# Branch C's attention steps in a 2-layer hybrid decoder: two places a unit instead of three, and a map factor made by one fused instruction

## What is computed

```python
def diff_attention(q, k, v, lam):
    """q,k [B,T,H,2,32]; v [B,T,H,64]; lam scalar -> (softmax1 - lam*softmax2) v, [B,T,H,64]."""
    ...
        s = jnp.einsum('bqhcd,bkhcd->bhcqk', qb, k).astype(jnp.float32) * scale
        p = jax.nn.softmax(jnp.where(causal, s, -jnp.inf), axis=-1)
        pd = (p[:, :, 0] - lam * p[:, :, 1]).astype(v.dtype)
        return jnp.einsum('bhqk,bkhd->bqhd', pd, v)
...
u = jnp.einsum('btnc,ncd->btnd', y, w_branch)
g = jax.nn.sigmoid(pr['g'].reshape(b, t, N_BRANCH, d))
out = jnp.sum(g * u, axis=2) @ w_out
return layer_norm(DN_ALPHA * x + out, ln_g, ln_b)
```

## Time and profile before

| | us |
|---|---|
| median of 3 runs | 1393.51 |
| lowest and highest | 1391.75, 1394.14 |
| the profiled execution | 1390.51 |
| its span | 1388.9 |
| PE busy | 1325.7 (95%) |
| DVE busy | 655.3 (47%) |
| ACT busy | 651.6 (47%) |
| POOL busy | 674.3 (49%) |

### The profile page before, as it was taken

How to read it: one execution, slowest core, us unless ns; L and a number is a source line. 1 busy time by engine, 2 the same in 40 slices (tenths; PEclk the granted TensorE clock), 3 DMA queues, 4 the chain that set the end, 5 groups by cost and what they waited for, 6 DMA issues and landing times.

```text
span 1388.9 us, 19055 instructions
## 1 busy us (share of the span) xinstructions
PE 1325.7 (95%) x6872; PEld 1126.4 (81%) x6872; DVE 655.3 (47%) x1641; ACT 651.6 (47%) x1296; POOL 674.3 (49%) x850
## 2 busy tenths in 40 slices
PE   6999999999999999999999989999999999999995
PEld 5977788888877898888888778888888779888884
DVE  4567746433146553213365774763322675432044
ACT  4455345454276464433245533554524764553232
POOL 3543353354565354467374325424446533645764
PEclk9999999999999999999999999999999999999998
DMA  7322242221331143242322113322124212323221
GB/s 263 109 74 62 70 114 68 65 74 62 103 95 38 39 119 106 58 121 76 119 76 86 61 61 88 95 76 74 57 64 116 61 45 80 96 58 106 84 76 60
DMA packets 147052, 116.47 MB, mean 84 GB/s; under 512 B 5520, under 2 KB 131856, under 8 KB 146704
## 3 DMA queue, kind: packets, MB, share of 16 engines
q1 hardware_dynamic: 146816, 114.22, 27.6%
q10 hardware_dynamic: 144, 1.05, 0.2%
HBM read 112.10 MB, written 3.15 MB: 83 GB/s over the span
## 4 chain that ended last, share of the span: by engine, by line
PE 81%; DVE 10%; ACT 4%; issue 2%; POOL 1%; DMA 1%; SPq 0%; POOLq 0%; DVEq 0%; ACTq 0%
PE product L729 20%; PE product L730 19%; PE product L731 19%; PE context L969 4%; PE scores L941 3%; PE branch_product L729 3%; PE branch_product L731 3%; PE branch_product L730 3%; PE transposed L954 3%; DVE probabilities L1398 1%; DVE index_scores L1364 1%; ACT score_operands L993 1%; DMA residual<-in_x_dram 1%; DVE index_scores L1375 1%; POOL residual L671 1%
## 5 line engine op out<-in xcount | busy, mean ns | idle before, releaser
L713 POOL TENSOR_TENSOR weights_rest<-raw_weights,weights_head 128x320 fp32r<-128x320 f32 (+3 forms) x672 | 544.3, 843 | 387.1 <-ACT weights_head L993 387.1
L729 PE MATMUL product<-weights_head,stationary_head 128*128 128x512 f32 (+3 forms) x768 | 291.2, 379 | 5.9 <-POOL weights_rest L713 5.8
L993 ACT ACTIVATE weights_head<-raw_weights 128x1280 fp32r<-128x1280 f32 (+4 forms) x178 | 198.1, 1114 | 206.6 <-PE product L731 160.9
L730 PE MATMUL product<-weights_rest,stationary_head 128*128 128x512 f32 (+3 forms) x768 | 286.0, 372 | 0.0
L731 PE MATMUL product<-weights_head,stationary_rest 128*128 128x512 f32 (+3 forms) x768 | 285.8, 372 | 0.0
L729 PE MATMUL product<-stationary_head,weights_head 128*128 128x512 f32 x640 | 260.6, 407 | 0.0
L730 PE MATMUL product<-stationary_rest,weights_head 128*128 128x512 f32 x640 | 250.4, 391 | 0.0
L731 PE MATMUL product<-stationary_head,weights_rest 128*128 128x512 f32 x640 | 250.4, 391 | 0.0
L698 POOL TENSOR_TENSOR merged<-merged,activated 128x256 f32<-128x256 f32 x128 | 93.2, 750 | 276.0 <-DVE activated L1519 275.9
L729 PEld LDWEIGHTS product<-weights_head,stationary_head 128*128 128x128 f32 x768 | 145.5, 189 | 27.6 <-POOL weights_rest L713 6.6
L1104 ACT ACTIVATE probabilities<-probabilities,negated_maxima 128x256 f32<-128x256 f32 (+3 forms) x160 | 86.3, 539 | 172.9 <-DVE negated_maxima L1398 172.2
(11 more groups left out here) (201 smaller groups left out, 1809.0 us busy)
## 6 DMA issues: line engine op xcount, KB each, us to landing
raw_weights<-in_w_in_dram SPq DMA_DIRECT2D x104, 512.0 KB, 3.7
raw_weights<-in_w_in_dram SPq DMA_DIRECT2D x72, 256.0 KB, 2.9
raw_weights<-in_w_branch_dram SPq DMA_DIRECT2D x80, 128.0 KB, 3.7
raw_weights<-in_w_out_dram SPq DMA_DIRECT2D x16, 512.0 KB, 3.6
merged<-in_w_mem_kv_dram SPq DMA_DIRECT2D x8, 512.0 KB, 7.3
raw_weights<-in_w_in_dram SPq DMA_DIRECT2D x8, 416.0 KB, 3.1
raw_weights<-in_w_in_dram SPq DMA_DIRECT2D x8, 296.0 KB, 3.9
residual<-in_x_dram SPq DMA_DIRECT2D x4, 512.0 KB, 10.7
```

The costliest lines, as they stand in the source:

```text
L713: ins = nc.gpsimd.tensor_tensor(WL[:, sw, part], RAW[:, sr, part], WH[:, sw, part].bitcast(F32), ALU.subtract)
L729: nc.tensor.matmul(dst, sh, mh, start=start, stop=False)
L730: nc.tensor.matmul(dst, sh, ml, start=False, stop=False)
L993: return nc.scalar.activation(dst, src, ACT.Copy, scale=scale)
```

## The change

The second and third place of a unit become one, so a unit has two places. The stretch of C's list ends one group of D0 later. The first factor step and the multiplication by lambda become one scalar_tensor_tensor: (1/r1 x lambda) x r0.

```diff
@@ diff_steps
         if j < NH and m < 2 and i < UNITS:
             third.append(("ev", "C", j, m))
             late = [("er", "C", j, m)]
-        out += [first, second, third]
+        out += [first, second + third]
     return out
@@ PLACES
-    ("C attention", ("gA0", 0, 0), ("D0", 3, 1), 0.0),
+    ("C attention", ("gA0", 0, 0), ("D0", 3, 2), 0.0),
@@ the join on DVE
                         chain(nc.vector.reciprocal(f[1], rs[1]))
-                        chain(nc.vector.tensor_tensor(f[0], f[1], rs[0], ALU.mult))
-                        chain(nc.vector.tensor_tensor(f[1], f[0], LAM[:, 4:5], ALU.mult))
-                        nc.vector.scalar_tensor_tensor(out=first, in0=second, scalar=f[1], in1=first, op0=ALU.mult,
+                        chain(nc.vector.scalar_tensor_tensor(out=f[0], in0=f[1], scalar=LAM[:, 4:5], in1=rs[0], op0=ALU.mult,
+                                                             op1=ALU.mult))
+                        nc.vector.scalar_tensor_tensor(out=first, in0=second, scalar=f[0], in1=first, op0=ALU.mult,
                                                        op1=ALU.add).then_inc(joined.sem, note(joined, step))
```

## The result

| | before | changed |
|---|---|---|
| median, us | 1392.63 | 1400.66 |
| lowest and highest, us | 1388.57, 1394.14 | 1400.04, 1402.86 |
| the profiled execution, us | 1390.51 | 1400.29 |
| its span, us | 1388.9 | 1398.7 |

The ratio is 1.0067, with a 95% interval of 1.0048 to 1.0087. The change made the kernel slower by 8 us. The forecast was 1394.9 us, from 1390.3 to 1398.4; it counted from a median before of 1393.51 us, and the one measured beside the changed kernel is 1392.63.

What follows compares the result with a forecast made beforehand. PE, busy 95% of the span, was taken as the bound. Old waits of 9.8 us a layer give way to 10.5, so +0.7 a layer and +1.4 on the median 1393.51: 1394.9 us, range 1390.3 to 1398.4.

Steps and rivals of the forecast that it cites:

- What bounds the kernel: Whole kernel: PE is busy 95% of the span, so time is lost or won where PE stands still.
- What goes: C's attention: the old waits for exits, joins and remainders leave their old places, a loss of 9.8 us a layer.
- What comes: C's attention: new waits at joins 0, 2, 4, 6, 8, following exits, remainders and the normaliser, 10.5 us a layer.
- ACT's 0.25: Units 2 and 6: ACT's remainder copies ahead of L1165 make L1519 0 to 0.6 us late, taken as 0.25 twice.
- second rival: ACT's copies hold L1519 at two places in each layer: 2.8 us more, 1397.7 us; chance 0.24.
- the sign of the forecast: PE in C's stretches: idle time near 7.6 us again, one of the signs that the forecast is right.
- The sum: C's attention, both layers: +0.7 us a layer, so +1.4 for the kernel, from -2 to +4.4.
- The waits' cost: PE's waits in C: start-to-start excess, 0.6 and 1.15 us at shared places, 0.2 more than their idle time.
- The fused step: DVE's joins in C: one factor step takes 0.20 us free and 0.77 behind L1519.
- The first rival: Five joins behind L1519 slip past POOL's pieces: 1385.6 us, or about 1390 with one delay gone; chance 0.16.
- The range: Kernel time to hold 8 in 10: 1390.3 to 1398.4 us, to the first rival's weak form and the second.

Runs made afterwards that it cites:

- the pauses filled: The changed kernel with matmuls of no use put into PE's long waits, before the transposes of units 2 and 6 and maps 8 and 16: 1394.96 us.
- the order alone: The changed kernel's order with the old join of two factor steps instead of the fused one: 1412.92 us, ratio 1.0138 to the kernel before.
- join first: The changed kernel with the join one place earlier, in the first place of the unit behind the even map's exit: 1384.57 us, ratio 0.9944.
- three places, new end: The changed kernel with three places a unit again, keeping the fused join and the stretch one group longer: 1381.98 us, ratio 0.9944.
- filled before maps 8 and 16: The changed kernel with 12 matmuls of no use before each of these two maps only, transpose pauses left empty: 1394.18 us, ratio 1.0017.
- remainders earlier: The changed kernel with q and k of each head prepared one unit earlier (ACT's copies and branch C's remainders): 1395.15 us, ratio 1.0025.
- join first, remainders earlier: The changed kernel with the join in the first place and the preparation one unit earlier: 1381.45 us, ratio 0.9930.

## Why the prediction was wrong

**What bounds the kernel** held: PE, so that time is lost or won where it stands still. That it can also run slower was left out.

**What goes** held. All 8 waits for exits are gone from their places but a rest at map 15 (0.17 us idle in layer 1, none in layer 0), and so are those at joins 11 and 13 and map 24.

**What comes** held in place, and in size but for unit 2. The waits stand at transposes 0, 2, 4, 6, 8 and maps 8, 16, where they were forecast. Forecast and measured (idle plus 0.16): 1.35 and 1.24 at unit 0; 1.10, with ACT's 0.25 1.35, and 1.94 at unit 2; 1.35 and 1.21 at unit 6; 1.8 and 1.70 at map 8; 0.52 and 0.41 at units 4 and 8; 0.7 and 0.59 at map 23. The join behind L1519 took 0.71 + 1.05 us where 0.77 + 1.12 was said: one wait for POOL in each, as worked out from the earlier trace rows. At unit 2 the term that was too small was ACT's: L1519 came 1.45 us after the last branch matmul, so 0.95 late, where I took 0.25 of a bound of 0.6; at unit 6 it was 0.58 late. The copies of 2.42 us ended at 414.02 and L1165 followed at 414.04:

```profile
411.60 2.42 ACT L993 ACTIVATE score_operands<-product 32x512 fp32r<-32x512 f32 x4
414.04 0.60 ACT L1165 ACTIVATE activated<-product 128x512 f32<-128x512 f32 x1
```

That is the second rival's mechanism, and at unit 2 its size too: 0.7 beyond what was taken. One of its signs is there as well, L1519 waiting for L1165 by over 1 us (1.68). In full it was priced at 2.8 us, to 1397.7, so it does not reach the measured time, and since the maps behind exits lost less than forecast, the idle sum came out at 7.9, near the 7.6 that was named as the sign of the forecast.

**The sum** is where it failed. "The waits' cost" was each wait's start-to-start excess, added up; no term stood for what the matmuls after a wait cost. The rows that would have warned were all there: the forecast itself put 1.1 + 1.8 us of waiting around a few small transposes before map 8. The trace of before has single waits up to 1.0 us in C, at full clock throughout; I carried that clock over to pauses three times as long. The waits' part was sized at +1.4 us. By the prediction's own measure the waits of the changed kernel come to 7.9 + 8 x 0.16 = 9.2 us in layer 0, against 9.8 before, so a little less than none was lost there; with the pauses filled +2.4 us are left (1394.96 against 1392.54, interval -0.1 to +2.9). The forecast lies between, and no run measures this part more closely. The missing term is 5.7 us by the filled kernel's median (1400.66 against 1394.96), up to 8 by the clock of the profile. Two slips in the sums carry no weight: the join that ends at 3.18 us is taken at 3.13 for map 8, and -2 and +4.4 us around 1393.51 are 1391.5 to 1397.9, where 1392.2 to 1397.7 stands.

**The fused step** was taken at 0.20 us and is 0.22 when free:

```profile
L1451 DVE SCALAR_TENSOR_TENSOR map_factors<-map_factors,lambdas,row_sums x32: 218/714/855, 404.9 to 1169.0; 128x1 f32<-128x1 f32 x32
```

Its median is 0.71: in the new order more than half of the fused steps meet POOL. The saving at joins that wait for POOL was right in kind: with the order alone each of the five joins holds PE 0.9 us longer.

**The first rival** (slipping past POOL) did not happen at any of the five. **The range** ended at 1398.4 since it held one rival at a time, and none that makes the same work slower.

## What to carry to other kernels

Add up PE's waits where they stand, not only in total: two waits with a few small matmuls between them can act as one long pause, so look at the granted clock of the stretch behind them, and behind long single waits too. Moving a step to break such a pair was worth more here than its idle time (5.5 us for 1.3); filling the pause with matmuls of no use is a cheap test of whether the clock is the cause. And where a list is dealt evenly over groups, its length and its end decide which step falls on which group: read the dealt order (which engine has its own long work in that group) before judging an entry more or less. Here the cost of two places instead of three was 7.5 or 18.7 us, by where the list ended.

## What was not expected of the hardware

- After PE was busy for 1.05 of 4 us (and again 1.55 of 4) its clock was granted at 0.5. Single waits of up to 1.0 us, in the kernel before, left it at 1.00 in C's stretch. Between 1.6 and 2.0 us the length of a single wait did not decide: behind 1.60 us (join first) the clock fell in both layers, behind 1.75 (three places, new end) in one, behind 1.79 (filled before maps 8 and 16) in neither, behind 1.97 (remainders earlier) in both. What else decides is open.
- One kernel's executions differed by 12.0 us (1379.1 to 1391.2), and their mean clock (0.992 to 0.983) went with it. It does not always: join first, remainders earlier ran at 1381.7 us with 0.986 and at 1381.2 with 0.991, and the kernel before at 1386.7 and 1391.7 with 0.992. A median of few runs of such a kernel says less than its interval suggests; the mean clock beside each time is a hint, not a measure.
- Fillers of 256 columns into the free half of a bank in use cost nothing measurable in waits that were there anyway: 4.43 us against 4.41.
